# Attention scores as three rounded products of high and low parts, in place of one full float32 product

## The chip, the cores and the metric

One core of a Trainium2 chip runs the whole program in one launch. The metric is the device time in microseconds (us), the median of several executions; lower is better.

## The reference

One decoder layer over 512 tokens of width 1024, in float32. The part that matters here is the attention of `nsa_mixer`: eight heads of 64, in two groups of four that share keys and values. With 512 tokens, eight selectable blocks of 64 and a top-8 selection, the selected branch is plain causal attention over `k_s`, and the window branch is causal attention over `k_w`. Both score the same normed queries:

```
q = rms_norm(q) * gain            # per head, 64 wide
s_s = q @ k_s.T * scale + bias    # then masked softmax, @ v_s
s_w = q @ k_w.T * scale + bias    # then masked softmax, @ v_w
s_c = q @ k_cmp.T * scale + bias  # 31 compressed blocks
out = gate0 * o_c + gate1 * o_s + gate2 * o_w
```

Around it stand the input projections, a gated linear recurrence, gates, an output projection and a squared-ReLU MLP.

## The kernel before, in words

Five engines run hand-written programs, each in a fixed order, and hand over by semaphores. The names used below are TensorE (PE), VectorE (DVE), ScalarE (ACT), GpSimd (POOL) and SyncE (SP). Every big product is made from rounded operands of the type `F32R`: a float32 matrix is stored as a rounded part (`...hi`) and the rounded rest (`...lo`), and `three` (L383) issues three matmuls per block of 128 rows (L385 to L387). SP loads one weight chunk of 128x1024 at a time, POOL splits it into two slots (`split`: L303 makes the high part, L305 subtracts it from the raw weights to get the low part), and `project` (L389) on PE multiplies eight blocks, 24 matmuls of 512 columns. PE releases a slot of weights with `w_used`, and POOL then begins the split of the chunk after the next.

The stage around the change runs in this order on PE.

- The compressed branch: `c_scores(qb)` (L684) makes scores against 31 compressed keys for the query block `qb`, a projection of a gate (`ga5`, `ga6`, `ga7`, `gb0`) follows, and then `c_turn(qb)` (L694) transposes the weights `pc`, for which it waits for `cp_scaled` from DVE. So the softmax of block `qb` has the length of one projection to get done. On DVE it is `c_shift` (L1403 to L1410: bias, row minimum, subtraction) and `c_weight` (L1418 to L1423), with an exponential on ACT between (L1041), and before it DVE empties the bank of the gate projected last (`gate`, L1154). The whole is preceded on DVE by the last low part of the recurrence's output (`oa_low`, L1368) and a memset of `pc` (L1385), and on ACT by the last high part (L1032).
- The attention proper: 32 rounds `t`, one for each pair of heads (one head of either group), branch (`ksn` or `kwn`) and query block `qb = t % 4`. `scores(t)` (L709) makes two score tiles of 128x`n`, where `n` is 128, 256, 384 or 512, with the two heads on rows 0 to 63 and 64 to 127 of the array and in two PSUM banks. The operands `qn`, `ksn` and `kwn` are plain float32. DVE adds the bias and finds the row minimum (`shift`, L1436), ACT takes the exponential (L1070), DVE inverts the sums (L1443), POOL scales (L348), and PE transposes the round three before (`turn`, L731) and multiplies the round pair five before with the values (`values`, L752). Six gate projections `gb2` to `gb7` are mixed in at rounds 3, 7, 13, 19, 30 and 32 to 34. The projection `gb1` stands between `scores(0)` and `scores(1)`.

After it come the branch projections (`ab0` to `ab7`), the output projection and the MLP, all with `three`.

Of the kernel before, what the change touches and what calls it, by code (L numbers as in the profile page):

```python
# [25 lines left out]
F32 = mybir.dt.float32  # L26
F32R = mybir.dt.float32r
U8 = mybir.dt.uint8
ACT = mybir.ActivationFunctionType
ALU = mybir.AluOpType  # L30
AX_X = mybir.AxisListType.X

P = 128
D = 1024
S = 512
# [44 lines left out]
def build_block(nc, xT, w, oh, masks, ident_in, small_in, w2, rel, scratch, skewed, out):  # L80
    with ExitStack() as ctx:
        base = (nc.sbuf_base + 31) // 32 * 32

        def at(name, kb, shape, dt=F32):

            return nc.alloc_sbuf_tensor_at(name, shape, dt, offset=base + int(kb * 1024))

        def sem(name):
            return ctx.enter_context(nc.semaphore(name))
# [36 lines left out]
        qn = at("qn", 160.5, [P, 4, S])  # L126
        ksn = at("ksn", 168.5, [P, S])
        kwn = at("kwn", 170.5, [P, S])
# [3 lines left out]
        sq = at("sq", 180.5, [P, 2, S])  # L132
        rstd = at("rstd", 184.5, [P, 2, S])
        tmp = at("tmp", 188.5, [P, S])
        oblo = at("oblo", 190.5, [P, 4, S], F32R)
        pt_low = [at("pt_low0", 186.5, [P, 2, 2, 256]), at("pt_low1", 198.5, [P, 2, 2, 256])]
        pt_high = [at("pt_high0", 116.5, [P, 2, 4, 256]), at("pt_high1", 178.5, [P, 2, 4, 256])]
        cst = at("cst", 204.5, [P, 336])
# [87 lines left out]
        normed = sem("normed")  # L226
# [2 lines left out]
        cexp, csum = sem("cexp"), sem("csum")  # L229
        hraw_ready, folded = sem("hraw_ready"), sem("folded")  # L230
        gel_ready, cmp_out, kcn_ready, vc_ready = (sem(n) for n in ("gel_ready", "cmp_out", "kcn_ready", "vc_ready"))
        cs_done, cs_shift, cp_ready, cp_scaled, cpT_done, cpT_copied = (
            sem(n) for n in ("cs_done", "cs_shift", "cp_ready", "cp_scaled", "cpT_done", "cpT_copied"))
        s_done = [sem("s_done0"), sem("s_done1")]
        s_shift = [sem("s_shift0"), sem("s_shift1")]
# [26 lines left out]

        def bank_of(name):
            return bank[USE[name] % 2]

        def score_bank(t, g):
            return bank[((2, 3), (1, 7))[t % 2][g]]
# [101 lines left out]
        def _(pe):  # L369
# [6 lines left out]
            def claim(name):  # L376

                n = USE[name]
                if n >= 2:
                    pe.wait_ge(free[n % 2], n // 2)  # L380
                return bank[n % 2]

            def three(out_, wh, wl, mh, ml, first, last):  # L383

                pe.matmul(out_, wh, mh, start=first, stop=False)  # L385
                pe.matmul(out_, wh, ml, start=False, stop=False)  # L386
                return pe.matmul(out_, wl, mh, start=False, stop=last)  # L387
# [271 lines left out]
            for g in range(2):  # L659
                for j in range(4):  # L660
                    last = pe.matmul(to[32 * j:32 * j + 32, g * 64:g * 64 + 64], gel[1][:, g * 32:g * 32 + 32],
                                     w2_v, start=True, stop=True, skip_group_check=True)
# [31 lines left out]
                    last = pe.transpose(bank[4][:, g * P:g * P + P], pc[:, g * P:g * P + P], ident[:])  # L694
                last.then_inc(cpT_done, 1)

            keys = (ksn, kwn)

            def scores(t):
                gi, qb = divmod(t, 4)  # L700
                i, b = divmod(gi, 2)
                n = (qb + 1) * P
                if t == 1:
                    claim(FIRST_PAD)
                for g in range(2):
                    rows = slice(64 * g, 64 * g + 64)
                    if t >= 2:
                        pe.wait_ge(s_shift[g], t - 1)
                    pe.matmul(score_bank(t, g)[:, 0:n], qn[rows, i, qb * P:qb * P + P], keys[b][rows, 0:n],  # L709
                              start=True, stop=True).then_inc(s_done[g], 1)  # L710

            c_scores(0)
            for qb, name in enumerate(("ga5", "ga6", "ga7", "gb0")):
# [73 lines left out]
            for n in range(KT):  # L787
                wh, wl = take(f"ab{n}")
                for j, (hi, lo) in enumerate(((oahi, oalo), (obhi, oblo))):
# [7 lines left out]
                    for k in range(4):  # L797
                        c = slice((4 * j + k) * P, (4 * j + k + 1) * P)
                        last = three(to[:], wh[:, c], wl[:, c], hi[:, k, :], lo[:, k, :], k == 0, k == 3)
# [22 lines left out]
            for half in range(HALVES):  # L822
# [14 lines left out]
                with pe.Fori(0, KT // 2) as i:  # L837
                    for j in range(2):
                        b = (r0 + j) % 2
                        pe.wait_ge(free[b], i + (r0 + j) // 2)  # L840
                        for part in range(2):
                            slot = (c0 + 2 * j + part) % NSPLIT
                            pe.wait_ge(w_split, 4 * i + (c0 + 2 * j + part + 1))
                            for k in range(8):
                                kk = 8 * part + k
                                if j == 0:
                                    pe.wait_ge(u_lo, half * UP_T + kk + 1)
                                c = slice(k * P, k * P + P)
                                last = three(bank[b][:], whi[:, slot, c], wlo[:, slot, c], uhi[:, kk, :],
                                             ulo[:, kk, :], kk == 0, kk == 15)  # L850
# [4 lines left out]
        def _(act):  # L855
# [14 lines left out]
            def inverse_rms(name, dim, n=S):  # L870

                outs[0] += 1
                act.wait_ge(stat_out, outs[0])
                to = rstd[:, rs[0] % 2, 0:n] if name != "stat_x" else rx[:]
                source = bank_of(name) if name != "stat_x" else bank[5]
                if rs[0] >= 2:
                    act.wait_ge(rs_used, rs[0] - 1)
                link(act.activation(to, source[:, 0:n], ACT.Ln, scale=1.0 / dim, bias=eps))
                if name != "stat_x":
                    act.sem_inc(free[USE[name] % 2], 1)  # L880
                act.activation(to, to, ACT.Exp, scale=-0.5).then_inc(rs_ready, 1)
                rs[0] += 1
                return to
# [86 lines left out]
            for j in range(4):  # L970
                rows, c = slice(32 * j, 32 * j + 32), slice(32 * j, 32 * j + 32)
                last = act.activation(sc[rows, :, 0:4, c], near[rows, :, :].rearrange("p (h t) c -> p h t c", h=HG),
                                      ACT.Copy)
# [32 lines left out]
            gelu_exp(0)  # L1006
            act.wait_ge(cmp_out, 1)
            link(act.activation(hid[:, 0, :], bank_of("cmp_k")[:, 0:64], ACT.Copy))
            link(act.activation(hid[:, 7, :], bank_of("cmp_k")[:, 0:64], ACT.Square))
            act.sem_inc(free[USE["cmp_k"] % 2], 1)  # L1010
# [4 lines left out]
            def square_o(h):  # L1015
                act.wait_ge(o_done, h + 1)
                act.wait_ge(stat_out, 7 if h < 2 else 7 + h)
                act.activation(sq[:, h % 2, :], bank[2 + h][:], ACT.Square).then_inc(stat_in, 1)
# [8 lines left out]
            for h in range(HG):  # L1027
                inverse_rms(f"st_o{h}", P)
                if h < 2:
                    square_o(h + 2)  # L1030
                act.wait_ge(oa_f, h + 1)
                act.activation(oahi[:, h, :], o_ring[:, h % 2, :], ACT.Copy).then_inc(oa_hi, 1)  # L1032
                if h == 0:
                    act.wait_ge(skew_out, 16)
                    act.dma_start(bias[:], skewed.rearrange("h p u -> p h u")).then_inc(bias_in, 16)

            for qb in range(ST):
                act.wait_ge(cs_shift, qb + 1)
# [4 lines left out]
                for g in range(2):  # L1043
                    last = act.activation(pcT[g][:, qb * P:qb * P + P], bank[4][:, g * P:g * P + P], ACT.Copy)
# [17 lines left out]
            for t in range(NT + VALUES - 1):  # L1062
                if LAG <= t < NT + LAG:
                    evacuate(t - LAG)
                if t < NT:
                    n = (t % 4 + 1) * P
# [30 lines left out]
            for half in range(HALVES):  # L1097
# [3 lines left out]
                with act.Fori(0, UP_T // 4) as i:  # L1101
                    for j in range(4):
                        b, s = (r0 + j) % 2, j % 2
# [11 lines left out]
        def _(dve):  # L1115
# [36 lines left out]
            def scaled(name, to):  # L1152
                dve.wait_ge(w_used, AT[name] + 1)
                link(dve.tensor_tensor(to, bank_of(name)[:], rx[:], ALU.mult))  # L1154
                dve.sem_inc(free[USE[name] % 2], 1)
# [127 lines left out]
            for j in range(2):  # L1283
# [3 lines left out]
                last = dve.tensor_tensor(xsp[j][:, :, 1, NCMP:32], pos_, xsp[j][:, :, 0, NCMP:32].bitcast(F32),  # L1287
                                         ALU.subtract)
# [56 lines left out]
            for g in range(2):  # L1345
                rows = slice(64 * g, 64 * g + 64)
                last = dve.scalar_tensor_tensor(kcn[rows, :], hid[rows, 0, 32 * g:32 * g + 32], g_kc[rows, :],
                                                rs_[rows, 32 * g:32 * g + 32], ALU.mult, ALU.mult)
# [5 lines left out]
            def gate(name):  # L1354
                scaled(name, gates[:, "ab".index(name[1]), int(name[2]), :])
# [32 lines left out]
            def by_head(v):  # L1388
                return v.rearrange("p (h one) -> p h one", one=1)
# [22 lines left out]
            def c_weight(qb):  # L1412
# [9 lines left out]
                link(dve.tensor_tensor(by_head(wc), by_head(wc), g3[:, :, 0:1], ALU.mult))  # L1422
                dve.tensor_tensor(pcv, pcv, by_head(wc).broadcast_to([P, NH, nc_]), ALU.mult).then_inc(cp_scaled, 1)  # L1423

            gate("ga4")
            for qb in range(ST):
                c_shift(qb)
# [2 lines left out]
            def shift(t, g):  # L1430
                gi, qb = divmod(t, 4)
                n = (qb + 1) * P
                dve.wait_ge(s_done[g], t + 1)
                if t >= 4:
                    dve.wait_ge(t_done[g], t - 3)
                dve.tensor_tensor_reduce(  # L1436
                    out=p_tile(t, g, n), in0=score_bank(t, g)[:, 0:n], in1=bias[:, 4 * g + gi // 2, S - n:S],
                    scale=1.0, scalar=3.0e38, op0=ALU.add, op1=ALU.min, accum_out=mins[:, t % 4, g:g + 1]
                ).then_inc(s_shift[g], 1)

            def invert(t):
                dve.wait_ge(p_exp, 2 * t + 2)
                dve.reciprocal(rinv[:, t % 4, :], sums[:, t % 4, :]).then_inc(w_ready, 1)  # L1443

            shift(0, 0)
            shift(0, 1)
            invert(0)
            gate("gb1")

            def evacuate(t):  # L1450
# [74 lines left out]
            for half in range(HALVES):  # L1525
# [3 lines left out]
                with dve.Fori(0, UP_T // 4) as i:  # L1529
                    for j in range(4):  # L1530
                        b, s = (r0 + j) % 2, j % 2
# [10 lines left out]
                with dve.Fori(0, KT // 2) as i:  # L1542
                    for j in range(2):
                        b = (r0 + j) % 2
# [120 lines left out]
```

## Time and profile before

| | before |
|---|---|
| median of 3 runs | 806.27 us (805.99 to 806.63) |
| the profiled execution, its own time | 806.03 us |
| span of the profiled core | 804.3 us |
| granted TensorE clock, mean | 0.999 |
| PE busy | 797.1 us (99%) |
| PE weight loads busy | 635.8 us (79%) |
| DVE busy | 396.2 us (49%) |
| ACT busy | 196.3 us (24%) |
| POOL busy | 489.1 us (61%) |

The profile is one execution recorded by the hardware. Its span runs from the first to the last instruction, and the execution's own time is 1.7 us more. Busy times overlap between engines. A float32 matmul shows as two records, an `F32R` matmul as one. The profile prints the types of matmul operands as f32 in both cases. A matmul record includes its latency, so records of one engine overlap, and the pace is the distance between starts.

### The profile page before, as it was taken

What the parts mean: (1) busy time and instruction counts of PE and PEld (TensorE: products, weight loads), DVE (VectorE), ACT (ScalarE), POOL (GpSimd) and SP (SyncE); (2) the same over time, 40 slices, a digit from 0 to 9 for tenths busy, and PEclk for the clock granted to TensorE, in tenths of its full rate; (3) what the DMA queues carried; (4) which work ended last, traced back from release to release, by engine and by line L of the source; (5) the groups of instructions that cost most, each with busy time, mean ns of one, the idle gap of its engine ahead of it and who ended that gap; (6) DMA issues with size and microseconds to landing.
All of it is one profiled execution on the core that took longest, in us unless ns stands there. A gap on an engine that the chain in (4) does not pass through costs nothing.

```text
span 804.3 us, 12357 instructions
## 1 busy us (share of the span) xinstructions
PE 797.1 (99%) x4632; PEld 635.8 (79%) x4632; DVE 396.2 (49%) x565; ACT 196.3 (24%) x402; POOL 489.1 (61%) x325
## 2 busy tenths in 40 slices
PE   9999999999999999999999999999999999999998
PEld 7788878988787666577888888888888888888886
DVE  5794577734465445633457667661000476650000
ACT  6101753214311445725112222220000122210000
POOL 5666544676454755555666566676666676676663
PEclk9999999999999999999999999999999999999999
DMA  8244222233522010015223223233223223323320
GB/s 282 98 139 154 82 80 80 79 106 105 183 79 78 27 53 28 1 53 183 84 101 104 89 95 104 80 102 105 84 99 104 82 102 104 98 85 131 130 78 26
DMA packets 23549, 78.01 MB, mean 97 GB/s; under 512 B 2723, under 2 KB 3499, under 8 KB 23380
## 3 DMA queue, kind: packets, MB, share of 16 engines
q1 hardware_dynamic: 19964, 69.00, 25.8%
q10 hardware_dynamic: 3544, 8.44, 2.9%
q8 instruction: 29, 0.48, 0.3%
q14 instruction: 12, 0.10, 0.0%
HBM read 75.31 MB, written 4.21 MB: 99 GB/s over the span
## 4 chain that ended last, share of the span: by engine, by line
PE 96%; ACT 1%; POOL 1%; DMA 1%; DVE 1%; issue 0%; SPq 0%; DVEq 0%; POOLq 0%; ACTq 0%
PE bank L385 27%; PE bank L387 26%; PE bank L386 26%; PE bank L709 3%; PE bank L731 3%; PE bank L752 2%; PE bank L467 1%; PE bank L468 1%; PE bank L469 1%; PE bank L409 1%; ACT gates L1081 1%; PE bank L516 1%; DMA x<-in_xT 1%; POOL wsp L305 1%; PE bank L625 1%; PE bank L741 1%
## 5 line engine op out<-in xcount | busy, mean ns | idle before, releaser
L305 POOL TENSOR_TENSOR wsp<-wraw,wsp 128x1024 fp32r<-128x1024 f32 x124 | 305.8, 2466 | 10.3
L303 POOL TENSOR_SCALAR wsp<-wraw 128x1024 fp32r<-128x1024 f32 x124 | 135.3, 1091 | 243.7 <-PE bank L387 159.2
L385 PE MATMUL bank<-hhi,wsp 128*128 128x512 f32 x352 | 140.6, 399 | 0.9 <-POOL wsp L305 0.4
L386 PE MATMUL bank<-hlo,wsp 128*128 128x512 f32 x352 | 137.3, 390 | 0.0
L387 PE MATMUL bank<-hhi,wsp 128*128 128x512 f32 x352 | 137.3, 390 | 0.0
L385 PE MATMUL bank<-ghi,wsp 128*128 128x512 f32 x256 | 100.4, 392 | 0.0
L387 PE MATMUL bank<-ghi,wsp 128*128 128x512 f32 x256 | 99.7, 389 | 0.0
L385 PE MATMUL bank<-uhi,wsp 128*128 128x512 f32 x256 | 99.7, 389 | 0.0
L386 PE MATMUL bank<-glo,wsp 128*128 128x512 f32 x256 | 99.6, 389 | 0.0
L386 PE MATMUL bank<-ulo,wsp 128*128 128x512 f32 x256 | 99.6, 389 | 0.0
L387 PE MATMUL bank<-uhi,wsp 128*128 128x512 f32 x256 | 99.6, 389 | 0.0
L385 PEld LDWEIGHTS bank<-hhi,wsp 128*128 128x128 f32 x352 | 66.0, 188 | 18.8 <-issue 3.5
L387 PEld LDWEIGHTS bank<-hhi,wsp 128*128 128x128 f32 x352 | 66.1, 188 | 14.2
L386 PEld LDWEIGHTS bank<-hlo,wsp 128*128 128x128 f32 x352 | 66.1, 188 | 12.5
L1535 DVE TENSOR_TENSOR u_ring<-t_ring,r_ring 128x512 f32<-128x512 f32 x32 | 57.2, 1789 | 1.1
L385 PEld LDWEIGHTS bank<-ghi,wsp 128*128 128x128 f32 x256 | 48.0, 188 | 11.8 <-issue 1.5
L387 PEld LDWEIGHTS bank<-ghi,wsp 128*128 128x128 f32 x256 | 48.1, 188 | 10.2
L385 PEld LDWEIGHTS bank<-uhi,wsp 128*128 128x128 f32 x256 | 48.1, 188 | 10.1 <-issue 0.3
L387 PEld LDWEIGHTS bank<-uhi,wsp 128*128 128x128 f32 x256 | 48.1, 188 | 10.1
L386 PEld LDWEIGHTS bank<-ulo,wsp 128*128 128x128 f32 x256 | 48.1, 188 | 10.0
L386 PEld LDWEIGHTS bank<-glo,wsp 128*128 128x128 f32 x256 | 48.1, 188 | 9.8 <-issue 0.2
L1538 DVE TENSOR_TENSOR ulo<-u_ring,uhi 128x512 f32 x32 | 38.6, 1206 | 32.5 <-ACT uhi L1107 32.5
(246 smaller groups left out, 1012.1 us busy)
## 6 DMA issues: line engine op xcount, KB each, us to landing
wraw<-in_w SPq DMA_DIRECT2D x126, 512.0 KB, 3.3
bias_skewed<-bias_lines ACTq DMA_DIRECT2D x1, 2048.0 KB
bias<-bias_skewed ACTq DMA_DIRECT2D x1, 2048.0 KB, 8.7
x<-in_xT ACTq DMA_DIRECT2D x1, 2048.0 KB, 8.1
out<-x ACTq DMA_DIRECT2D x8, 256.0 KB, 2.0
x<-in_xT SPq DMA_DIRECT2D x3, 512.0 KB, 6.6
x<-in_xT SPq DMA_DIRECT2D x2, 256.0 KB, 4.4
wraw<-in_w SPq DMA_DIRECT2D x4, 128.0 KB, 8.0
```

The costliest lines, as they stand in the source:

```text
L303: pool.tensor_scalar(whi[:, two, :], wraw[:, raw, :], 1.0, 0.0, ALU.mult, ALU.add).then_inc(w_hi, 1)
L305: pool.tensor_tensor(wlo[:, two, :], wraw[:, raw, :], whi[:, two, :].bitcast(F32), ALU.subtract).then_inc(w_split, 1)
L385: pe.matmul(out_, wh, mh, start=first, stop=False)
L386: pe.matmul(out_, wh, ml, start=False, stop=False)
L387: return pe.matmul(out_, wl, mh, start=False, stop=last)
L409: pe.matmul(to[:, 0:n], matrix, squares, start=True, stop=True).then_inc(stat_out, 1)
L467: pe.matmul(to, hh, wh[:, c], start=k == 0, stop=False)
L709: pe.matmul(score_bank(t, g)[:, 0:n], qn[rows, i, qb * P:qb * P + P], keys[b][rows, 0:n], start=True, stop=True).then_inc(s_done[g], 1)
L731: last = pe.transpose(bank[4 + g][:, kb * P:kb * P + P], p_tile(t, g, S)[:, kb * P:kb * P + P], ident[:])
L752: last = pe.matmul(bank[6][64 * g:64 * g + 64, 256 * half + c:256 * half + 256], v_sw[:, kb, b * P + g * 64:b * P + g * 64 + 64], pt[:, g, ...
L1535: dve.tensor_tensor(u_ring[:, s, :], t_ring[:, s, :], r_ring[:, s, :], ALU.mult).then_inc(u_f, 1)
L1538: dve.tensor_tensor(ulo[:, 4 * i + j, :], u_ring[:, s, :], uhi[:, 4 * i + j, :].bitcast(F32), ALU.subtract).then_inc(u_lo, 1)
```

## The change

`qn` is split into `q_high` and a low part, `ksn` and `kwn` into `k_high` and `k_low`, all of type `F32R`. ACT makes the six high parts as rounded copies of 128x512 after the last `oahi` and before the first exponential of the compressed branch. DVE makes the low parts by subtraction, two for the keys and two for the first two query tiles between the memset of `pc` and `gate("ga4")`, and the other two between `invert(0)` and `gate("gb1")`. `scores(t)` then issues high x high, high x low and low x high, each for both heads in turn, accumulated in the same bank. `oblo` moves to the place of `qn`, whose data is dead by then. `keys` goes.

```diff
-        oblo = at("oblo", 190.5, [P, 4, S], F32R)
+        oblo = at("oblo", 160.5, [P, 4, S], F32R)
+        q_high = at("q_high", 136.5, [P, 4, S], F32R)
+        q_low_early = at("q_low_early", 190.5, [P, 2, S], F32R)
+        q_low_late = at("q_low_late", 164.5, [P, 2, S], F32R)
+        k_high = at("k_high", 194.5, [P, 2, S], F32R)
+        k_low = at("k_low", 168.5, [P, 2, S], F32R)
...
+        def q_low(i):
+            return q_low_early[:, i, :] if i < 2 else q_low_late[:, i - 2, :]
...
                 if t == 1:
                     claim(FIRST_PAD)
-                for g in range(2):
-                    rows = slice(64 * g, 64 * g + 64)
-                    if t >= 2:
-                        pe.wait_ge(s_shift[g], t - 1)
-                    pe.matmul(score_bank(t, g)[:, 0:n], qn[rows, i, qb * P:qb * P + P], keys[b][rows, 0:n],
-                              start=True, stop=True).then_inc(s_done[g], 1)
+                if t % 8 == 0:
+                    pe.wait_ge(q_lo, i + 1)
+                if t == 0:
+                    pe.wait_ge(k_lo, 2)
+                c = slice(qb * P, qb * P + P)
+                for part, (q_, k_) in enumerate(((q_high[:, i, c], k_high[:, b, 0:n]), (q_high[:, i, c], k_low[:, b, 0:n]),
+                                                 (q_low(i)[:, c], k_high[:, b, 0:n]))):
+                    for g in range(2):
+                        rows = slice(64 * g, 64 * g + 64)
+                        if t >= 2 and part == 0:
+                            pe.wait_ge(s_shift[g], t - 1)
+                        last = pe.matmul(score_bank(t, g)[:, 0:n], q_[rows, :], k_[rows, :], start=part == 0,
+                                         stop=part == 2)
+                        if part == 2:
+                            last.then_inc(s_done[g], 1)
...
+            act.wait_ge(normed, 6)
+            for b in range(2):
+                act.activation(k_high[:, b, :], (ksn, kwn)[b][:], ACT.Copy).then_inc(k_hi, 1)
+            for i in range(4):
+                act.activation(q_high[:, i, :], qn[:, i, :], ACT.Copy).then_inc(q_hi, 1)
...
+            for b in range(2):
+                dve.wait_ge(k_hi, b + 1)
+                dve.tensor_tensor(k_low[:, b, :], (ksn, kwn)[b][:], k_high[:, b, :].bitcast(F32),
+                                  ALU.subtract).then_inc(k_lo, 1)
+
+            def query_low(i):
+                dve.wait_ge(q_hi, i + 1)
+                dve.tensor_tensor(q_low(i), qn[:, i, :], q_high[:, i, :].bitcast(F32), ALU.subtract).then_inc(q_lo, 1)
+
+            query_low(0)
+            query_low(1)
             gate("ga4")
...
             invert(0)
+            query_low(2)
+            query_low(3)
             gate("gb1")
```

The order on DVE at the place of the first four subtractions, before the change. `pc` holds the compressed scores, `cst` the row minima and sums, `gates` the gate projections.

```order
L1368 TENSOR_TENSOR oalo<-o_ring,oahi 128x512 [waits oa_hi] x2
L1385 MEMSET pc 128x256
L1154 TENSOR_TENSOR gates<-bank,rx 128x512 [waits w_used,dve_step]
L1403 TENSOR_TENSOR pc<-bank,bias 128x4x7 [waits dve_step,bias_in,cs_done]
L1407 TENSOR_REDUCE cst<-pc 128x8 [waits dve_step]
L1408 TENSOR_TENSOR pc<-pc,cst 128x8x7 [waits dve_step]
L1410 TENSOR_SCALAR cst<-cst 128x8 [waits dve_step]
L1418 TENSOR_REDUCE cst<-pc 128x8 [waits cp_ready]
```

With the change, the same place.

```order
L1390 TENSOR_TENSOR oalo<-o_ring,oahi 128x512 [waits oa_hi] x2
L1407 MEMSET pc 128x256
L1449 TENSOR_TENSOR k_low<-ksn,k_high 128x512 [waits k_hi,dve_step]
L1449 TENSOR_TENSOR k_low<-kwn,k_high 128x512 [waits k_hi]
L1454 TENSOR_TENSOR q_low_early<-qn,q_high 128x512 [waits q_hi] x2
L1176 TENSOR_TENSOR gates<-bank,rx 128x512 [waits w_used,dve_step]
L1425 TENSOR_TENSOR pc<-bank,bias 128x4x7 [waits dve_step,bias_in,cs_done]
```

Four subtractions of 128x512 now stand ahead of the emptying of `ga4` and so ahead of the first softmax of the compressed branch.

On PE, the first round of scores before the change, with the transposition ahead of it.

```order
L694 MATMUL bank<-ident,pc 128x128
L709 MATMUL bank<-ksn,qn 128x128 [waits cs_shift]
L709 MATMUL bank<-ksn,qn 128x128
L385 MATMUL bank<-hhi,wsp 128x512 [waits bank0_read,w_split]
L386 MATMUL bank<-hlo,wsp 128x512
```

With the change.

```order
L703 MATMUL bank<-ident,pc 128x128
L723 MATMUL bank<-k_high,q_high 128x128 [waits k_lo,q_lo,cs_shift]
L723 MATMUL bank<-k_high,q_high 128x128
L723 MATMUL bank<-k_low,q_high 128x128 x2
L723 MATMUL bank<-k_high,q_low_early 128x128 x2
L394 MATMUL bank<-hhi,wsp 128x512 [waits bank0_read,w_split]
```

Two float32 matmuls became six `F32R` matmuls, and the round waits for the low parts as well. The other 31 rounds change in the same way.

## Rows read from the trace of the kernel before

**Rows 1.** The page: the chain that ended last, by engine

```profile
PE 96%; ACT 1%; POOL 1%; DMA 1%; DVE 1%; issue 0%; SPq 0%; DVEq 0%; POOLq 0%; ACTq 0%
```

**Rows 2.** A stretch of four rounds: its length, then busy PE, PEld, DVE, ACT, POOL

```profile
306.00:314.20 8.20, 8.20 (x62) 4.86 (x60) 5.74 (x24) 6.16 (x21) 4.79 (x9) 1.00 0.01 3
```

**Rows 3.** Timeline of PE in that stretch: start us, length us, instruction

```profile
306.03 0.49 PE L709 MATMUL bank<-ksn,qn 64*128 64x128 f32 x4
306.45 0.66 PE L731 MATMUL bank<-ident,p_ring 128*128 128x128 f32 x4
307.04 0.70 PE L709 MATMUL bank<-ksn,qn 64*128 64x256 f32 x4
307.67 0.88 PE L731 MATMUL bank<-ident,p_ring 128*128 128x128 f32 x6
...
311.15 1.13 PE L709 MATMUL bank<-ksn,qn 64*128 64x512 f32 x4
312.21 0.44 PE L731 MATMUL bank<-ident,p_ring 128*128 128x128 f32 x2
```

**Rows 4.** Timeline of PE: the compressed scores, and rounded matmuls of 512 columns behind

```profile
225.36 1.08 PE L684 MATMUL bank<-kcn,qn 64*128 64x31 f32 x16
226.37 0.50 PE L385 MATMUL bank<-hhi,wsp 128*128 128x512 f32 x1
226.71 0.40 PE L386 MATMUL bank<-hlo,wsp 128*128 128x512 f32 x1
226.94 0.39 PE L387 MATMUL bank<-hhi,wsp 128*128 128x512 f32 x1
```

**Rows 5.** Timeline of PE: eight rounded matmuls of 256 columns, and what follows

```profile
167.87 1.12 PE L606 MATMUL bank<-wsp,xsp_k 128*128 128x256 f32 x8
168.83 1.48 PE L625 MATMUL bank<-sc,v_i 128*128 128x128 f32 x9
```

**Rows 6.** Timeline of DVE where the first four subtractions go

```profile
222.94 1.47 DVE L1368 TENSOR_TENSOR oalo<-o_ring,oahi 128x512 fp32r<-128x512 f32 x2
224.41 0.27 DVE L1385 MEMSET pc<- 128x256 f32 x1
225.54 0.69 DVE L1154 TENSOR_TENSOR gates<-bank,rx 128x512 f32<-128x512 f32 x1 [0.85 <-PE bank L387]
...
227.10 2.09 DVE L1408 TENSOR_TENSOR pc<-pc,cst 128x56 f32<-128x56 f32 x1
229.35 0.17 DVE L1410 TENSOR_SCALAR cst<-cst 128x8 f32<-128x8 f32 x1 [0.16 <-DVE pc L1408]
...
230.45 0.22 DVE L1423 TENSOR_TENSOR pc<-pc,cst 128x56 f32<-128x56 f32 x1
```

**Rows 7.** Timeline of POOL in the same stretch

```profile
225.59 1.05 POOL L303 TENSOR_SCALAR wsp<-wraw 128x1024 fp32r<-128x1024 f32 x1 [3.12 <-PE bank L387]
226.72 2.40 POOL L305 TENSOR_TENSOR wsp<-wraw,wsp 128x1024 fp32r<-128x1024 f32 x1
232.27 1.05 POOL L303 TENSOR_SCALAR wsp<-wraw 128x1024 fp32r<-128x1024 f32 x1 [3.15 <-PE bank L387]
```

**Rows 8.** Timeline of ACT: the last high part before the new copies

```profile
223.05 0.63 ACT L1032 ACTIVATE oahi<-o_ring 128x512 fp32r<-128x512 f32 x1 [1.95 <-DVE o_ring L1381]
```

**Rows 9.** Timeline of DVE and of POOL where the two meet earlier in the kernel

```profile
152.93 2.06 DVE L1232 TENSOR_TENSOR q_dec<-q_dec,tot 128x1024 f32<-128x1024 f32 x1
...
152.83 1.08 POOL L303 TENSOR_SCALAR wsp<-wraw 128x1024 fp32r<-128x1024 f32 x1 [0.98 <-PE bank L469]
153.99 3.25 POOL L305 TENSOR_TENSOR wsp<-wraw,wsp 128x1024 fp32r<-128x1024 f32 x1
```

**Rows 10.** Timeline of PE: the first transposition of the compressed branch

```profile
231.94 0.38 PE L694 MATMUL bank<-ident,pc 128*128 128x128 f32 x2
```

**Rows 11.** Timeline of PE: float32 matmuls of 128 columns at the very start

```profile
1.68 6.68 PE L442 MATMUL bank<-ones 128*128 128x128 f32 x32 [1.68 <-DVE relx L1133]
8.11 0.47 PE L385 MATMUL bank<-hhi,wsp 128*128 128x512 f32 x1
```

More of the change, by code:

```diff
@@ L231, in build_block @@
         gel_ready, cmp_out, kcn_ready, vc_ready = (sem(n) for n in ("gel_ready", "cmp_out", "kcn_ready", "vc_ready"))
+        k_hi, k_lo, q_hi, q_lo = sem("k_hi"), sem("k_lo"), sem("q_hi"), sem("q_lo")
         cs_done, cs_shift, cp_ready, cp_scaled, cpT_done, cpT_copied = (
@@ L695, in c_turn @@
                 last.then_inc(cpT_done, 1)
-            keys = (ksn, kwn)
             def scores(t):
```

## The prediction

> **What bounds the kernel now.** I read the chain that ended last first: 96% of it is TensorE [rows 1]. What PE gains or loses in a stretch is therefore gained or lost in the whole. A stretch of four attention rounds without a projection shows the same: PE is busy for all 8.20 us, DVE for 5.74, ACT for 6.16 and POOL for 4.79 [rows 2]. So other engines matter only where PE comes to a wait and they are late. I then read the pace of a round of scores from the distances between starts [rows 3], the pace of rounded matmuls [rows 4, 5], and last the place where the high and low parts are made, on DVE, POOL, ACT and PE [rows 6 to 10].
>
> After the change a round has three passes for each head, in six matmuls with six weight loads. I assume the heads stay side by side. With 512 columns: 0.2 fixed + 3 x 0.23 = 0.89. With 384: 0.2 + 3 x 0.17 = 0.71. With few columns the loads decide. The compressed scores have 64x128 loads as well and only 31 columns, and 16 load-and-matmul records take 1.01 us [rows 4], 0.126 for a pair of heads. So 256 columns, whose pass is 0.107, take 0.2 + 2 x 0.126 + 0.107 = 0.56, and 128 columns 0.2 + 2 x 0.126 + 0.053 = 0.51. Four rounds fall from 2.96 (0.42 + 0.63 + 0.85 + 1.06) to 2.67, and the 32 rounds by 8 x 0.29 = **2.3 us**. I take 1.9, because a round's transposes and the scores two rounds later wait for DVE, ACT and POOL, which have little more than 2 us of slack in 8.2 [rows 2] and do not get faster.
>
> The bounds. No rounded matmul under 256 columns is in this trace; with 256 a step takes 0.12, eight in 0.96 [rows 5], near one pass. If a rounded 128-column matmul had to make four passes, its round would take 0.2 + 3 x 0.21 = 0.84 in place of 0.51, and eight of them 2.6 us more: the scores would come out at -2.3 + 2.6 = +0.3. One pass less of four without any extra cost of loads would save 0.053 x (1 + 2 + 3 + 4) = 0.53 in four rounds, 4.3 in all. So the scores lie between -4.3 and +0.3, and I stay in the middle.
>
> What a load costs is where a rule speaks against the change. The sixteen records above allow at most 0.063 for one load with its matmul. The Trainium skill, TensorE: Matmul & The Clock Gate, section LDWEIGHTS (loading the stationary operand), gives the load's time as its columns over 1.2 per ns, which is 107 ns here whatever the rows. If six such loads came one after the other, a round would not go below 0.84, the scores would cost 8 x 0.45 = 3.6 us instead of saving 1.9, and the sum would be 814.7. The row speaks against it, and I leave its rival a small chance.
>
> **The high parts.** ACT makes six copies of 0.63 us. It ends its last high part at 223.68 [rows 8] and would be through with all six by about 227.4. Its next work, the exponential of L1041, waits for the subtraction L1408, which ends at 229.19 [rows 6]. Cost nothing; without that cover each copy would be 0.63.
>
> **The first four low parts are the other large term.** DVE takes 0.68 us for such a subtraction (L1368, two in 1.47 [rows 6]), but they have both inputs in SBUF, and such an operation does not run beside POOL. L1408, a subtraction of 56 columns whose sister L1423 takes 0.22, takes 2.09: it starts at 227.10 and ends at 229.19, when L305 ends at 229.12 [rows 6, 7]. It also goes the other way, by turns: L1232 starts at 152.93 while POOL's L303 runs to 153.91, ends only at 154.99, and the L305 behind it takes 3.25 instead of 2.40 [rows 9]. So I put the engines in turn:
>
> - memset ends at 224.68. `k_low` 0 and 1 run to 226.07. L303, due at 225.59, waits for them and ends at about 227.05.
> - `q_low` 0 goes next, to 227.7. L305 has waited and runs to 230.1. `q_low` 1 waits for it and ends at 230.75.
> - The emptying of `ga4` (0.69), which started at 225.54 before, ends at 231.5. The bias, reduction and subtraction of `c_shift(0)` end near 232.3.
> - PE has finished `ga5` by then, and the next L303 is due at 232.27 [rows 7] as before, with L305 behind it. The weights of the softmax have three operations with two SBUF inputs (L1420, L1422, L1423). They fall into these 3.5 us, and only the first gets a turn: L305 runs from about 233.5 to 235.9, and `cp_scaled` comes at about 236.5. If L1408 itself loses to L303, it is 237.3.
>
> Before, it came at 230.67, and PE asked at 231.94 [rows 6, 10]. The slack of 1.27 us is gone and PE waits 4.6 to 5.4 us: I take **4.9**. It happens once. POOL's next split needs the end of `ga6`, so the later softmaxes have their old places relative to PE, and the DVE's chain of 4.2 us (226.5 to 230.7, with its long L1408) fits the 5.6 between. `ga6` needs its bank at the earliest when `ga4` has been emptied, 231.5, and PE is then still in `ga5`. POOL's delayed split of 3.5 us ends at 230.1, before PE needs it at about 232.3.
>
> **The other low parts** stand behind `invert(0)`, where DVE has nothing to do until PE has finished `gb1`, 24 matmuls at 0.23 or 5.5 us. Two subtractions of 0.68, with at most one L305 of 2.40 ahead of them, fit in. Cost nothing; `oblo` and the three semaphore waits on PE cost nothing either, since the parts are ready long before.
>
> **The sum** against the profiled execution: 806.0 + 4.9 - 1.9 = 809.0 us. The median shown is 0.24 above that execution, so 809.2.
>
> **The rivals.**
>
> - *The low parts slip through.* If DVE keeps its turn for all four (226.07, then on to 227.5, with POOL waiting), the softmax is done close to 231.9 and PE waits little or not. Then the gain remains: 806.3 - 1.9 = 804.4, down to 802 with the full 4.3. For it: the result hangs on who gets the next turn. Against it: in [rows 9] POOL got in each time that it had waited. It decides when `q_low` 1 starts before 228.0. A partial case, L1408 or L1423 held once, loses 1.5 to 2 us and lands at 806.
> - *PE's clock falls in the wait.* The granted clock is full, 2.4 GHz, throughout this trace, and PE has no wait of such a length in it after its start. Its first 32 float32 records of 128 columns take 6.43 us [rows 11], 0.20 each, where two passes at the later pace are 0.107: half pace, the lower level of 1.2 GHz, after it had been idle. At most 3.2 us would be lost that way after a wait of 4.9: 812.4. The Trainium skill's same page, Part 1, says that an idle array is gated down to half until it has been busy for a while; by that rule the sum would be up to 3.2 higher.
> - *Loads, or short rounded matmuls, are dear.* A load is hidden under 0.12 us at 256 columns [rows 5], so it takes at most that. Six of those give 0.92 for every round, 3.68 for four, +5.8 in all, and with the wait 817. The short matmuls alone give 806.3 + 4.9 + 0.3 = 811.5.
> - *The heads no longer side by side.* Six passes of 512 columns would be 1.4 + 0.2 against 1.06. I see no reason in the operands' type, since the rows and banks stay.
>
> **How the numbers follow.** Wait of 4.6 to 5.4 with the gain of about 1.9: 0.50. The wait and a lower clock: 0.13. The wait with dear loads, short matmuls or heads in turn: 0.08. Partial wait: 0.11. No wait: 0.18. A measurement of this kernel can tell about 0.2%, 1.6 us, from no change. Below 804.7 lies most of the no-wait case, above 807.9 nearly all of the first three: faster 0.18, same 0.13, slower 0.69. The likeliest case alone spans 807 to 811. For 8 in 10 I go from 803.7 to 812.6.
>
> **What would show it.** PE idle before the first transposition (L694 before) for 4.6 to 5.4 us, released by DVE, with the second to fourth not waiting. The second `q_low` at over 2 us instead of 0.68, ending with L305. Start distances of the score rounds of 0.51, 0.56, 0.71 and 0.89. The granted clock at 1.00 right after the wait, or not. A span that has shrunk without that wait would make the forecast wrong, and so would a round of 128 columns above 0.8.

## The result, and the profile after

| | before | changed |
|---|---|---|
| median | 806.30 us (6 runs, 805.99 to 807.0) | 811.33 us (6 runs, 810.15 to 812.35) |
| ratio to before | | 1.006, 95% interval 1.005 to 1.007 |
| span of the profiled core | 804.3 us | 810.5 us |
| granted clock, mean | 0.999 | 0.996 |
| PE, DVE, ACT, POOL busy | 797.1, 396.2, 196.3, 489.1 us | 798.1, 402.9, 198.8, 489.9 us |

The changed kernel is slower by 5.0 us, 0.6%. The profiled execution took 812.35 us, 1.0 above the median. The chain that ended last shows what is new, against [rows 1]:

```profile
PE 94%; DVE 2%; ACT 2%; POOL 1%; DMA 1%; issue 0%; SPq 0%; DVEq 0%; POOLq 0%; ACTq 0%
```

PE no longer has 96% of the chain, and DVE and ACT have a per cent more each (a per cent of the span is about 8 us, and the shares are rounded). The starts on PE tell where. The table takes them from the timelines of the two kernels.

| start of | before | changed | stretch grew by |
|---|---|---|---|
| first compressed scores | 225.36 | 226.34 | +0.98 |
| first transposition | 231.94 | 236.84 | +3.92 |
| second transposition | 238.88 | 246.94 | +3.16 |
| first round of scores | 253.07 | 261.08 | -0.05 |
| branch projections | 362.53 | 368.31 | -2.23 |
| end of the span | 804.3 | 810.5 | +0.42 |

The 0.98 lies ahead of anything that the change touches. Most of it, 0.8 us, is there within the first 20 us, and in the profiles of the eight experiments the first compressed scores start between 225.2 and 225.9, so it belongs to this execution and not to the change. It is about the amount by which this execution is above its median. What the change did is three numbers: 3.92, a wait; 3.16, something right behind it; and -2.23, a gain in the attention. The last 0.42 has no cause that I can show. From the branch projections to the end the kernel before takes 441.8 us, and the changed kernel and the experiments whose profiles I compared (spread, float32 scores, three ahead, split held, two products) take 442.2 to 442.3. So it seems to come with the new kernel, and no run looked for it.

**The wait.** The timeline of DVE in the changed kernel (start us, length us), where [rows 6] stood before. L1449 and L1454 are the new subtractions, L1176 the gate, L1430, L1442, L1444 and L1445 were L1408, L1420, L1422 and L1423:

```profile
225.70 0.69 DVE L1449 TENSOR_TENSOR k_low<-ksn,k_high 128x512 fp32r<-128x512 f32 x1
226.31 0.68 DVE L1449 TENSOR_TENSOR k_low<-kwn,k_high 128x512 fp32r<-128x512 f32 x1
226.91 4.33 DVE L1454 TENSOR_TENSOR q_low_early<-qn,q_high 128x512 fp32r<-128x512 f32 x2
231.16 0.68 DVE L1176 TENSOR_TENSOR gates<-bank,rx 128x512 f32<-128x512 f32 x1
...
232.65 0.22 DVE L1430 TENSOR_TENSOR pc<-pc,cst 128x56 f32<-128x56 f32 x1
...
233.72 0.57 DVE L1442 TENSOR_TENSOR cst<-cst 128x8 f32<-128x8 f32 x1
234.33 0.17 DVE L1444 TENSOR_TENSOR cst<-cst 128x8 f32<-128x8 f32 x1
234.54 2.25 DVE L1445 TENSOR_TENSOR pc<-pc,cst 128x56 f32<-128x56 f32 x1
```

The timeline of POOL beside it, where [rows 7] stood:

```profile
226.57 1.33 POOL L312 TENSOR_SCALAR wsp<-wraw 128x1024 fp32r<-128x1024 f32 x1 [3.12 <-PE bank L396]
227.98 2.71 POOL L314 TENSOR_TENSOR wsp<-wraw,wsp 128x1024 fp32r<-128x1024 f32 x1
233.24 1.04 POOL L312 TENSOR_SCALAR wsp<-wraw 128x1024 fp32r<-128x1024 f32 x1 [2.56 <-PE bank L396]
234.37 2.34 POOL L314 TENSOR_TENSOR wsp<-wraw,wsp 128x1024 fp32r<-128x1024 f32 x1
```

The key parts take 0.7 each. L312 meets the second of them and takes 1.33 in place of 1.05, to 227.90. The first query part waits for L312 and goes next, L314 waits for that part and takes 2.71 in place of 2.40, to 230.69, and the second query part waits for L314 and ends at 231.24. So two subtractions of 0.68 took 4.33. The line shows the two together. How they share the time is my reading of POOL's lines, and the run with three subtractions ahead shows the first alone, at 1.52. The gate is emptied at 231.16, 4.6 us later than in [rows 6] once the 0.98 is taken off. The softmax then meets the next split. L1442 waits for L312 (0.57 in place of 0.17), L1444 slips in, and L1445, which took 0.22 before, stands behind L314, which ends at 236.71. The Trainium skill, SBUF — State Buffer, section Who interferes with whom, says that a VectorE instruction with two SBUF inputs contends with a GpSimd instruction that reads SBUF. The trace agrees, with 4.33 us for work of 1.4, and with the turns of [rows 9].

**Behind the wait.** The timeline of PE (the idle time before an instruction and what ended it in brackets), and behind it five stretches by window (start and end, length, then busy PE, PEld, DVE, ACT, POOL, the granted clock, the DMA share and GB/s):

```profile
236.84 0.61 PE L703 MATMUL bank<-ident,pc 128*128 128x128 f32 x2 [3.76 <-DVE pc L1445]
237.38 1.92 PE L693 MATMUL bank<-kcn,qn 64*128 64x31 f32 x16
...
240.25 0.63 PE L396 MATMUL bank<-hhi,wsp 128*128 128x512 f32 x1
240.68 0.63 PE L394 MATMUL bank<-hhi,wsp 128*128 128x512 f32 x1
...
243.96 0.39 PE L396 MATMUL bank<-hhi,wsp 128*128 128x512 f32 x1
244.19 0.39 PE L394 MATMUL bank<-hhi,wsp 128*128 128x512 f32 x1
```

```profile
232.00:236.00 4.00, 1.08 (x5) 0.56 (x3) 3.53 (x10) 0.25 (x1) 2.67 (x2) 1.00 0.34 121
236.00:237.00 1.00, 0.16 (x1) 0.16 (x2) 1.00 (x2) 0.00 (x0) 0.71 (x1) 0.98 0.00 0
237.00:238.00 1.00, 1.00 (x8) 0.67 (x9) 0.38 (x1) 0.45 (x2) 0.00 (x0) 0.50 0.25 41
...
243.00:244.00 1.00, 1.00 (x5) 0.76 (x4) 0.00 (x0) 0.00 (x0) 0.00 (x0) 0.60 0.00 0
244.00:245.00 1.00, 1.00 (x6) 0.83 (x5) 0.00 (x0) 0.00 (x0) 0.00 (x0) 1.00 0.00 0
```

The granted clock still stands at 1.00 while PE idles. It falls to 0.50, that is 1.2 GHz, at about 237, when PE has just begun again after 3.76 us without work. It stays there until about 243.8, with PE busy all the while, and then is 1.00 again. The matmuls of 512 columns step by 0.43 in place of 0.23, and the compressed scores take 1.85 in place of 1.01. That is the 3.16 us between the two transpositions, since PE waits for nothing in that stretch.

**The gain.** One round of 128 columns and one of 512 in the changed kernel, against [rows 3]. Each line holds one product for both heads:

```profile
313.03 0.33 PE L723 MATMUL bank<-k_high,q_high 64*128 64x128 f32 x2
313.19 0.27 PE L723 MATMUL bank<-k_low,q_high 64*128 64x128 f32 x2
313.31 0.27 PE L723 MATMUL bank<-k_high,q_low_late 64*128 64x128 f32 x2
313.51 0.66 PE L747 MATMUL bank<-ident,p_ring 128*128 128x128 f32 x4
...
318.00 0.50 PE L723 MATMUL bank<-k_high,q_high 64*128 64x512 f32 x2
318.34 0.39 PE L723 MATMUL bank<-k_low,q_high 64*128 64x512 f32 x2
318.56 0.40 PE L723 MATMUL bank<-k_high,q_low_late 64*128 64x512 f32 x2
318.89 0.44 PE L747 MATMUL bank<-ident,p_ring 128*128 128x128 f32 x2
```

The rounds take 0.48 and 0.89, and with 256 and 384 columns 0.56 and 0.72 (314.10 to 314.66, 316.26 to 316.98). Four sum to 2.65 against 2.96, so the 32 rounds have 2.5 us less to do, and 2.23 of that arrives (253.07 to 362.53 before, 261.08 to 368.31 now).

### The profile page after: what moved, and what is told of

Same layout as the page of the kernel before. It is cut to its first block, busy times and chain, and to the rows that moved or that the text cites. A ratio compares the mean times of both kernels' runs of the same rounds, so it can differ in the third digit from the quotient of the medians.

```text
span 810.5 us, 12501 instructions
## 1 busy us (share of the span) xinstructions
PE 798.1 (98%) x4696; PEld 641.1 (79%) x4696; DVE 402.9 (50%) x571; ACT 198.8 (25%) x408; POOL 489.9 (60%) x325
## 4 chain that ended last, share of the span: by engine, by line
PE 94%; DVE 2%; ACT 2%; POOL 1%; DMA 1%; issue 0%; SPq 0%; DVEq 0%; POOLq 0%; ACTq 0%
PE bank L394 26%; PE bank L396 25%; PE bank L395 25%; PE bank L747 3%; PE bank L723 3%; PE bank L768 2%; PE bank L476 1%; PE bank L477 1%; PE bank L478 1%; PE bank L418 1%; ACT gates L1103 1%; DMA x<-in_xT 1%; PE bank L525 1%; POOL wsp L314 1%; PE bank L634 1%; DVE q_low_early L1454 1%
## 5 line engine op out<-in xcount | busy, mean ns | idle before, releaser
L314 POOL TENSOR_TENSOR wsp<-wraw,wsp 128x1024 fp32r<-128x1024 f32 x124 | 305.6, 2464 | 10.3
L312 POOL TENSOR_SCALAR wsp<-wraw 128x1024 fp32r<-128x1024 f32 x124 | 135.7, 1094 | 251.1 <-PE bank L396 166.3
```

The costliest lines, as they stand in the source:

```text
L312: pool.tensor_scalar(whi[:, two, :], wraw[:, raw, :], 1.0, 0.0, ALU.mult, ALU.add).then_inc(w_hi, 1)
L314: pool.tensor_tensor(wlo[:, two, :], wraw[:, raw, :], whi[:, two, :].bitcast(F32), ALU.subtract).then_inc(w_split, 1)
```

## The experiments

Each ran on a chip beside runs of the kernel before, whose median was 806.09 us beside the first four experiments and 806.28 us beside the others. The ratios are taken against those. The edits are against the changed kernel, and ... marks what is left out. The theory (A in the texts): one wait, made by DVE and POOL taking turns, then PE at half clock, and a real gain in the rounds. The rivals are named in each.

### The parts spread out

```diff
-            for b in range(2):
+            def key_low(b):
...
-            query_low(0)
-            query_low(1)
             gate("ga4")
             for qb in range(ST):
                 c_shift(qb)
                 c_weight(qb)
+                if qb < 2:
+                    key_low(qb)
+                if qb == 2:
+                    query_low(0)
                 gate(("ga5", "ga6", "ga7", "gb0")[qb])
...
             invert(0)
+            query_low(1)
             query_low(2)
             query_low(3)
```

> The low parts are moved, nothing else: one after each of the first three softmaxes of the compressed branch (keys, keys, first query tile), the other three behind the inversion of round 0. Theory A (the loss is one wait of PE, made by VectorE and GpSimd taking turns, and the lower clock behind it): before each gate projection is emptied VectorE has been idle for over 1 us with GpSimd idle too, a subtraction of 0.68 fits, PE waits nowhere in the compressed branch, the clock stays up, and what remains is the gain of the scores: 2.0 to 2.5 us below before, some 804. Rival B (making the parts costs PE time wherever they stand, by the engines' load or by a second wait at the first round of scores): at or above before, 806 to 809.

Measured: 804.45 us (11 runs), ratio to before 0.9978, interval 0.9969 to 0.9987. That is 1.6 us faster than before and 6.9 faster than the change. DVE in this kernel:

```profile
230.72 0.22 DVE L1445 TENSOR_TENSOR pc<-pc,cst 128x56 f32<-128x56 f32 x1
230.86 0.68 DVE L1449 TENSOR_TENSOR k_low<-ksn,k_high 128x512 fp32r<-128x512 f32 x1
232.42 0.69 DVE L1176 TENSOR_TENSOR gates<-bank,rx 128x512 f32<-128x512 f32 x1 [0.88 <-PE bank L396]
```

The subtraction fits between the softmax and the end of PE's projection, and 0.88 us of idle time is left. The first transposition waits for nothing. The first round of scores starts at 253.35 and the branch projections at 360.62: 107.27, as in the changed kernel (107.23). So the gain is the same and only the loss is gone. B falls: making the parts costs PE nothing up to the branch projections. That the kernel gains 1.6 and not 2.2 goes with the 0.5 us behind them that I can't explain.

### PE kept busy in the wait

```diff
                 project(name)
+                if qb == 0:
+                    for _ in range(14):
+                        pe.matmul(bank[6][:], hhi[:, 0, 0:P], hhi[:, 0, :], start=True, stop=True)
                 c_turn(qb)
```

> The changed kernel with 14 rounded matmuls of 512 columns, whose result nobody reads, between the projection ga5 and the first transposition, where PE waits 3.9 us. At a step of 0.23 they take 3.2 of those. Theory A: the wait for VectorE ends when it did, but PE has been busy, the granted clock stays at 1.00, and the 3.1 us lost at half pace behind the wait come back: about 808. Rival B (the projection behind the wait is slow for another reason, the loads of weights or the late split): 811, or more where the 14 matmuls delay something.

Measured: 808.31 us (8 runs), ratio 1.0028, interval 1.0017 to 1.0039, 3.0 below the change, or 2.8 when each is taken against its own runs of before. PE in this kernel:

```profile
232.26 3.33 PE L733 MATMUL bank<-hhi 128*128 128x512 f32 x14
236.23 0.44 PE L703 MATMUL bank<-ident,pc 128*128 128x128 f32 x2 [0.64 <-DVE pc L1448]
...
238.17 0.40 PE L396 MATMUL bank<-hhi,wsp 128*128 128x512 f32 x1
238.41 0.40 PE L394 MATMUL bank<-hhi,wsp 128*128 128x512 f32 x1
```

The transposition still comes 3.97 us after the projection's end, so the wait is unchanged. The step behind it is 0.24 and the granted clock 1.00 in every window from 218 to 244. So matmuls whose result nobody reads made the kernel about 3 us faster. This separates the two losses: about 3.9 the wait, 2.8 to 3.2 the clock.

### Float32 scores with the parts made

```diff
-                if t % 8 == 0:
-                    pe.wait_ge(q_lo, i + 1)
+                if t == 0:
+                    pe.wait_ge(q_lo, 2)
+                if t == 1:
+                    pe.wait_ge(q_lo, 4)
...
-                for part, (q_, k_) in enumerate(...three products...):
-                    for g in range(2): ...
+                for g in range(2):
+                    rows = slice(64 * g, 64 * g + 64)
+                    if t >= 2:
+                        pe.wait_ge(s_shift[g], t - 1)
+                    pe.matmul(score_bank(t, g)[:, 0:n], q_low(i)[rows, c].bitcast(F32),
+                              k_low[rows, b, 0:n].bitcast(F32), start=True, stop=True).then_inc(s_done[g], 1)
```

> The parts are made as in the change, but each round is again one float32 product per head, of the low parts of queries and keys (the products with the high parts are left out). Theory A: the wait and the clock stay, the scores' gain of 2.2 us goes: 2.2 above the changed kernel, about 813.5, rounds at 0.42, 0.63, 0.85 and 1.06 again. Rival C (the rounded scores gain nothing in the whole, since other engines hold the rounds back, and the stretch got shorter for another reason): 811, as with the change.

This kernel leaves out the products with the high parts, so its scores are those of the low parts alone. Measured: 813.69 us (4 runs), ratio 1.0094, interval 1.0078 to 1.0109, 2.4 above the change, or 2.6 when each is taken against its own runs of before. The first round starts at 260.05 and the branch projections at 369.54: 109.49, against 109.46 before. So the gain of the rounds is 2.2 us by the traces and 2.4 to 2.6 by the medians. C falls.

### The heads one after the other

```diff
-                for part, (q_, k_) in enumerate(...):
-                    for g in range(2):
+                for g in range(2):
+                    for part, (q_, k_) in enumerate(...):
```

> The same six matmuls of a round in another order: the three of the first head, then the three of the second. Theory D (the heads run side by side only where their matmuls alternate, since PE starts its matmuls in order): only the third of one head and the first of the other overlap, five passes in a row in place of three, 0.2 + 5 x 0.23 = 1.35 with 512 columns and about 0.95 more over four rounds, +7.6 us in all: 819. Rival E (two heads' products of three passes overlap in any order, or are bound by the six weight loads): 811 as with the change.

Measured: 810.63 us (4 runs), ratio 1.0058, interval 1.0042 to 1.0073, as the change within their spread. D falls. A round of 512 columns:

```profile
293.57 0.51 PE L724 MATMUL bank<-k_high,q_high 64*128 64x512 f32 x2
293.91 0.41 PE L724 MATMUL bank<-k_low,q_high 64*128 64x512 f32 x2
294.15 0.40 PE L724 MATMUL bank<-k_high,q_low_early 64*128 64x512 f32 x2
294.49 0.44 PE L748 MATMUL bank<-ident,p_ring 128*128 128x128 f32 x2
```

The program has high x high, high x low and low x high of one head and only then those of the other. The records still pair the same product of both heads, and the round takes 0.92.

### Three subtractions ahead in place of four

```diff
             query_low(0)
-            query_low(1)
             gate("ga4")
...
             invert(0)
+            query_low(1)
             query_low(2)
```

> The changed kernel with one subtraction moved: the low part of the second query tile goes behind the inversion of round 0, three subtractions stay ahead of the emptying of ga4. Theory A (what costs is the turn that VectorE loses to a split of 2.4 us, twice): the gate is emptied about 2 us earlier, the softmax is done before GpSimd begins its next split, and PE waits nowhere: about 804, as with the parts spread. Rival B (each subtraction ahead of the softmax costs its own length): a quarter of the wait goes, about 1 us, and the clock still falls: 809 to 810.

Measured: 804.60 us (11 runs), ratio 0.9980, interval 0.9971 to 0.9989. Taking one subtraction of 0.68 away from this place takes away all of the loss. DVE in this kernel:

```profile
226.45 1.52 DVE L1454 TENSOR_TENSOR q_low_early<-qn,q_high 128x512 fp32r<-128x512 f32 x1
227.90 0.68 DVE L1176 TENSOR_TENSOR gates<-bank,rx 128x512 f32<-128x512 f32 x1
...
229.39 0.92 DVE L1430 TENSOR_TENSOR pc<-pc,cst 128x56 f32<-128x56 f32 x1
...
231.57 0.22 DVE L1445 TENSOR_TENSOR pc<-pc,cst 128x56 f32<-128x56 f32 x1
```

The softmax is done at 231.79, 0.66 before PE's transposition at 232.45, and L312 begins at 232.78. The query part has waited for L312, and L1430 for the end of L314, for which its like L1408 had waited 2.09 before [rows 6]. So the softmax is only 0.6 us later relative to PE, and the slack of 1.27 us takes that. With the fourth subtraction, that one stands behind the whole of L314, and the softmax comes so late that it meets the next split as well. B falls again.

### The split held back

```diff
             for c in range(3, AT["gb2"] + 1):
+                if c == AT["ga6"]:
+                    pool.wait_ge(cp_scaled, 1)
                 split_straight(c)
```

> The changed kernel, all four subtractions where they are, but GpSimd begins the split for the projection ga6 only when the first softmax is done. Theory A: no operation of VectorE meets GpSimd before that, the softmax is done 1 us or more before PE asks, and there is no wait at the transposition. GpSimd ends its split some 0.7 us after PE wants ga6. In all 804.5 to 805.5. Rival F (VectorE's chain is long in itself, whoever else uses the memory port): the wait at the transposition stays near 4 us and the late split comes on top: 812 or more.

Measured: 805.04 us (11 runs), ratio 0.9986, interval 0.9977 to 0.9995. DVE and then PE in this kernel:

```profile
226.02 1.29 DVE L1456 TENSOR_TENSOR q_low_early<-qn,q_high 128x512 fp32r<-128x512 f32 x2
```

```profile
234.06 0.50 PE L396 MATMUL bank<-hhi,wsp 128*128 128x512 f32 x1 [0.64 <-POOL wsp L314]
```

With all four subtractions in place and only POOL kept away, the two query parts take 1.29 in place of 4.33, and the transposition (232.04) waits for nothing. The price is the 0.64 that PE waits for the late split. F falls: the length came from the meeting with POOL.

### Two products

```diff
-                for part, (q_, k_) in enumerate(((q_high[:, i, c], k_high[:, b, 0:n]), (q_high[:, i, c], k_low[:, b, 0:n]),
+                for part, (q_, k_) in enumerate(((q_high[:, i, c], k_low[:, b, 0:n]),
...
-                                         stop=part == 2)
-                        if part == 2:
+                                         stop=part == 1)
+                        if part == 1:
```

> The changed kernel without the product of high and high: two rounded products per head in place of three. Theory A with passes: a round loses one pass, 0.23 at 512 columns, 0.17 at 384, and below 256 columns one pair of weight loads, about 0.12: rounds of 0.36, 0.44, 0.54 and 0.66, 8 x 0.65 = 5.2 us less on PE. Not all of it arrives, since VectorE and ScalarE have about 2 us of slack in 8: 807 to 808, against 811. Rival G (the rounds are no longer what holds this stretch): 811.

This kernel leaves out the product of high and high, the largest part of the scores. Measured: 808.52 us (7 runs), ratio 1.0026, interval 1.0015 to 1.0037, 2.8 below the change and a little above the 807 to 808 expected. The rounds take 0.37, 0.43, 0.55 and 0.67, in all 2.02 against 2.65, so PE has 5.0 us less to do. The stretch from the first round to the branch projections is 104.38 us against 107.23: 2.85 arrive, 57%. Of the change's own 2.5 us, 2.23 had arrived. G falls, but the rounds seem to be near the point where the other engines hold them: PE is idle for 1.36 us of that stretch, against 0.41 with the change.

### One head's products only

```diff
                     for g in range(2):
...
+                        if g == 1 and part < 2:
+                            continue
-                        last = pe.matmul(..., start=part == 0,
+                        last = pe.matmul(..., start=part == 0 or g == 1,
```

> The changed kernel, in which the second head of a round gets only its last product (low queries, high keys); its first two are left out. If the two heads' matmuls run side by side, a round of 512 columns keeps its three passes and 0.89, and short rounds lose a little where the weight loads hold them (four loads in place of six, 0.48 towards 0.40 at 128 columns). If they ran one behind the other, 512 columns would fall by two passes of 0.23.

This kernel leaves out two of the three products of the second head of each round. Measured: one run, 810.37 us, too few to compare times with, so I read the lengths of its rounds alone. A round of 128 columns, followed by its transposes:

```profile
288.64 0.32 PE L725 MATMUL bank<-k_high,q_high 64*128 64x128 f32 x1
288.65 0.32 PE L725 MATMUL bank<-k_high,q_low_early 64*128 64x128 f32 x1
288.80 0.27 PE L725 MATMUL bank<-k_low,q_high 64*128 64x128 f32 x1
288.92 0.27 PE L725 MATMUL bank<-k_high,q_low_early 64*128 64x128 f32 x1
289.12 0.66 PE L749 MATMUL bank<-ident,p_ring 128*128 128x128 f32 x4
```

With 512 columns the round still takes 0.89 (293.70 to 294.59): the heads run side by side. But with 128 it still takes 0.48 too, with four loads in place of six. So the loads of the two heads do not share one path either. The lines show one thing more. In the program both products of low queries and high keys stand behind high x low, and yet one of them starts at 288.65, ahead of the high x low at 288.80. So the second head's only product seems not to have waited for the first head's.

## Why the prediction was right, and where it was off

- **Direction and place: right.** The forecast was 809.2 with 803.7 to 812.6, the median is 811.33. It named the wait at the first transposition, its cause and the softmax operations that would meet the next split. Five runs bear it out: the spread parts, three in place of four and the held split for the wait, the fill for the clock, and the float32 scores for the gain.
- **The wait: 4.9 expected, 3.92 measured.** The step was "only the first gets a turn". DVE's chain was some 0.5 us earlier than I had put it. L1442 waited for L312 alone and L1444 got through, so that only L1445 stood behind L314 and ended 0.08 us after it. I had put two operations there, and their end 0.6 us after it. Another 0.3 is that I had gone above 4.6 for the case that the first subtraction of the softmax loses a turn too. It did not (L1430, 0.22).
- **The clock: the case that I left out of the sum.** I gave it 0.13 and at most 3.2 us. It happened and cost 3.16 by the trace, 2.8 to 3.0 by the run with the fill. This is the mis-sized part of the forecast: 1.0 too much for the wait, 3.2 too little for the clock. The two errors partly cancel, so the measured time lies nearer to 809.2 than the clock alone would have put it, and that is luck. The price had come from PE's first records [rows 11], and that price was right. What I misjudged was the chance: the granted clock fell to half in the changed kernel and in each of the four experiments that kept the wait and left PE idle in it, and it held at 1.00 in those that did not. The Trainium skill, TensorE: Matmul & The Clock Gate, Part 1, says that an idle array is gated down to half until it has been busy for a while. The trace agrees, with 0.50 granted from just after 3.76 us of idling.
- **The gain of the scores: right.** Rounds of 0.51, 0.56, 0.71 and 0.89 were expected, and 0.48, 0.56, 0.72 and 0.89 came. Of 2.3 us I had taken 1.9, and 2.23 arrived by the trace, 2.4 to 2.6 by the run with float32 scores. Rounded matmuls of 128 columns are not dear.
- **One reason in it was wrong.** I took the 0.126 of [rows 4] for a pair of heads, with two loads, one per head, in turn. But a float32 matmul shows as two records, so the 16 records are eight heads, and a pair of heads took four records and 0.25. The 0.126 is one record of either head, side by side. The run with one head's products shows the same 0.12 step with a single head at work, so it is the pace of one head, and the other's loads run beside it. By this the Trainium skill's 107 ns for a load of 128 columns (TensorE: Matmul & The Clock Gate, section LDWEIGHTS) agrees with the step of 0.11 to 0.12. So the 0.063 per load that I held against it was a misreading. The rival of six loads in a row fell for another reason: they come as two rows of three.
- **The rest.** The six copies on ACT (four in 2.17 us) and the late query parts cost PE nothing that shows up to the branch projections, as said. The 0.4 us behind them was in no term, and its cause stays open.

## What to carry to other kernels

Where two engines take turns, an operation moved into the slack of a chain can cost its turn, and not its length. Here the fourth subtraction, 0.68 us of VectorE work beside GpSimd splits of 2.4 us, turned the 0.66 us of slack that three had left into a wait of 3.9, while the same work further on was free. Look on the trace for stretches in which both engines are idle, and put it there. Price a wait on a full TensorE with the slow clock behind it, which here nearly doubled it.

## What the runs showed of the hardware that I had not expected

The matmuls of two row halves need not alternate in the program. With three of one head ahead of three of the other, a 512-column round took 0.92, against 0.89 with alternation, and the records show the same product of both heads at the same start. The Trainium skill, TensorE: Matmul & The Clock Gate, Part 3, section The mechanism, has matmuls start strictly in program order. The trace of that run differs, and five passes in a row would have been about 1.35 (my estimate, from passes of 0.23). The run with one head's products differs too: the second head's matmul starts at 288.65, though it stands last in the program, and the first head's second and third start at 288.80 and 288.92. So the two halves seem to work through queues of their own. That is how I read the starts of these two runs.

Loads for one half likewise do not hold up the other: a 128-column round took 0.48 with six loads and with four.
